# Second tile's norm by halves, one weight chunk reordered, and the input tokens issued on ScalarE's queue

## What is computed

```python
x = layer_norm(ALPHA * x + mix(x), ln_mix_g, ln_mix_b)          # mix: convolutions, then attention
x = layer_norm(ALPHA * x + moe(x), ln_ffn_g, ln_ffn_b)          # 32 experts, top 2 of one group
```

## Time and profile before

| what | value |
|---|---|
| median of 3 runs | 1653.17 us (1652.9 to 1653.77) |
| the profiled execution | 1655.15 us, span of its instructions 1653.4 us |
| mean granted TensorE clock | 0.995 |
| TensorE busy | 1564.0 us, 95% |
| VectorE / ScalarE / GpSimd busy | 482.5 / 266.7 / 72.0 us |
| DMA over the span | 502.48 MB, mean 304 GB/s |

### The profile page before, as it was taken

One profiled execution on the slowest core, in us unless ns is written; L12 is line 12 of the kernel. 1 busy time (PEld: TensorE's weight loads), 2 busy tenths in 40 slices (PEclk: granted clock), 3 DMA queues, 4 the chain that ended last, 5 costly groups with the idle time before them and its releaser, 6 DMA issues.

```text
span 1653.4 us, 25094 instructions
## 1 busy us (share of the span) xinstructions
PE 1564.0 (95%) x10686; PEld 1039.7 (63%) x10686; DVE 482.5 (29%) x934; ACT 266.7 (16%) x667; POOL 72.0 (4%) x138
## 2 busy tenths in 40 slices
PE   9999999998989999999999998898999999999999
PEld 8855555555555676465556555554888678748874
DVE  4951000000000313440000000002436887345652
ACT  1020000000000212210000000001232333322321
POOL 0000000000000000000000000000000431101120
PEclk9999999999999999999999999999999999999999
DMA  9689999999999942499999999999324223324420
GB/s 388 271 326 370 428 427 429 426 430 427 430 427 428 423 165 102 190 421 412 428 428 428 429 427 428 428 427 425 131 109 153 102 103 133 122 102 153 153 102 26
DMA packets 38661, 502.48 MB, mean 304 GB/s; under 512 B 4288, under 2 KB 4544, under 8 KB 6208
## 3 DMA queue, kind: packets, MB, share of 16 engines
q1 hardware_dynamic: 38016, 499.40, 73.3%
q0 software_dynamic: 576, 2.10, 0.3%
HBM read 500.43 MB, written 1.05 MB: 303 GB/s over the span
## 4 chain that ended last, share of the span: by engine, by line
PE 76%; DMA 12%; DVE 7%; issue 2%; ACT 2%; SPq 0%; DVEq 0%; ACTq 0%
PE ps L862 12%; PE ps L885 10%; PE ps L1320 10%; DMA ring<-in_expert_up 9%; PE ps L725 8%; PE ps L948 7%; PE ps L757 6%; PE ps L841 4%; PE ps L907 4%; DMA ring<-in_expert_down 3%; DVE arena L2263 2%; PE ps L1279 2%; PE ps L1107 2%; PE ps L1128 2%; PE ps L1401 1%
## 5 line engine op out<-in xcount | busy, mean ns | idle before, releaser
L862 PE MATMUL ps<-x_tok,tables_sb 128*128 128x256 f32 x1216 | 303.8, 393 | 0.0
L862 PEld LDWEIGHTS ps<-x_tok,tables_sb 128*128 128x128 f32 x1216 | 220.1, 191 | 103.9 <-issue 80.4
L885 PE MATMUL ps<-ring,arena 128*32 128x256 f32 x3968 | 238.6, 382 | 30.4 <-DMA ring<-in_expert_up 20.8
L885 PEld LDWEIGHTS ps<-ring,arena 128*32 128x32 f32 x3968 | 118.8, 110 | 139.0 <-issue 30.9
L725 PE MATMUL ps<-spare,ring 128*128 128x256 f32 x768 | 168.8, 383 | 1.1 <-DVE spare L2140 1.1
L2379 DVE TENSOR_TENSOR arena<-arena,ps 128x128 f32<-128x128 f32 x64 | 18.4, 288 | 497.2 <-ACT arena L1744 497.2
L725 PEld LDWEIGHTS ps<-spare,ring 128*128 128x128 f32 x768 | 147.0, 192 | 21.6 <-DVE spare L2140 1.3
L948 PE MATMUL ps<-ring,arena 128*32 128x512 f32 x928 | 115.6, 615 | 15.9 <-ACT arena L1739 11.3
L1320 PE MATMUL ps<-ring 128*128 128x256 f32 x480 | 110.6, 384 | 0.0
L1320 PEld LDWEIGHTS ps<-ring 128*128 128x128 f32 x480 | 89.8, 190 | 17.1 <-issue 5.5
L757 PE MATMUL ps<-ring,arena 128*128 128x512 f32 x224 | 98.6, 595 | 1.1 <-DVE arena L2315 0.6
(11 more groups left out here) (301 smaller groups left out, 1397.5 us busy)
## 6 DMA issues: line engine op xcount, KB each, us to landing
ring<-in_expert_up SPq DMA_DIRECT2D x124, 2048.0 KB, 20.6
ring<-in_stream SPq DMA_DIRECT2D x43, 2048.0 KB, 8.2
ring<-in_expert_down SPq DMA_DIRECT2D x42, 2048.0 KB, 24.1
ring<-in_expert_down SPq DMA_DIRECT2D x32, 1024.0 KB, 22.3
arena<-in_expert_up SPq DMA_DIRECT2D x4, 2048.0 KB, 11.2
arena<-in_expert_down SPq DMA_DIRECT2D x2, 2048.0 KB, 12.6
tables_sb<-in_expert_down SPq DMA_DIRECT2D x2, 2048.0 KB, 10.0
spare<-in_expert_down SPq DMA_DIRECT2D x2, 2048.0 KB, 10.3
```

Source lines behind the costliest of these rows:

```text
L862: pe.matmul(ps[:, b, 0:TOK], ident, x[:, 0, 0:TOK], start=True, stop=True, skip_group_check=True)
L885: ins = pe.matmul(ps[q * SLOTS:(q + 1) * SLOTS, 4 + e % 2, 0:TOK] .rearrange("p (g n) -> p g n", g=2), xg[:, 4 * half + k, e * SLOTS:(e + ...
```

## The change

- The two transfers of x are issued by ScalarE's queue, ahead of its other work, and no longer by SyncE's.
- In MOE1's opening order chunk 4 stands before chunk 10.
- CONV and STICK raise `half_done` when the first 512 columns of tile 1's output are summed; STICK's last three k-steps run first for these columns, then for the others. In CONV the order of matmuls stays.
- `layer_norm` of these stages takes tile 1's first half's statistics at that signal, and then does the passes over tile 1 by halves of 512 columns: subtract and gain, root, scale and bias of the first half, then of the second.
- In the expert stages the last two transposes of tile 1 (channel blocks 6 and 7) go to bank 4; VectorE copies 256 columns of bank 3, and ScalarE 256 of bank 4, in place of VectorE's 512.

```diff
@@ -178,8 +178,10 @@
         place_of[g], loads_of[g], before_in[g] = b, loaded[b], held.get(b)
         held[b] = g
 
-    halves = [(n, what) for n, what in ((CONV, "out"), (MOE0, "first"), (MOE0, "last"),
-                                        (STICK, "out"), (MOE1, "first"), (MOE1, "last"))
+    halves = [(n, what) for n, what in ((CONV, "out"), (CONV, "summed"),
+                                        (MOE0, "first"), (MOE0, "last"),
+                                        (STICK, "out"), (STICK, "summed"),
+                                        (MOE1, "first"), (MOE1, "last"))
               if n in on]
 
     def half_no(stage, what):
@@ -498,8 +500,6 @@
         @block.sync
         def _(sp):
             sp.dma_start(con[:, 0:P], a["tables"][:, 0:P]).then_inc(x_in, 16)
-            sp.dma_start(x[:, 0, :], a["x"][0][0:P, :]).then_inc(x_in, 16)
-            sp.dma_start(x[:, 1, :], a["x"][0][P:, :]).then_inc(x_late_in, 16)
 
             def load(g, src):
                 if before_in[g] is not None:
@@ -518,7 +518,7 @@
                 if stage == MOE0:
                     order = (7, 0, 1, 2, 3, 6, 8, 10, 4, 5, 9, 11)
                 else:
-                    order = (0, 1, 2, 3, 6, 10, 4, 7, 8, 5, 9, 11)
+                    order = (0, 1, 2, 3, 6, 4, 10, 7, 8, 5, 9, 11)
                 half = SLOT_WORDS // 2
                 for j in order:
                     if j == QUAD_CHUNKS - 1:
@@ -692,15 +692,18 @@
 
         @block.tensor
         def _(pe):
-            def transposes(name, src, ready=lambda t, kk: None, tiles=(0, 1), at=range(4)):
+            def transposes(name, src, ready=lambda t, kk: None, tiles=(0, 1), at=range(4),
+                           last_two=None):
 
                 for b in [2 * t + kk for t in tiles for kk in range(2)]:
                     t, kk = b // 2, b % 2
                     ready(t, kk)
                     for j in range(4):
                         k = 4 * kk + j
-                        ins = pe.transpose(bank(at[b])[:, j * P:(j + 1) * P],
-                                           src[:, t, k * P:(k + 1) * P], ident)
+                        o = bank(at[b])[:, j * P:(j + 1) * P]
+                        if k >= 6 and t and last_two is not None:
+                            o = bank(last_two)[:, (k - 6) * P:(k - 5) * P]
+                        ins = pe.transpose(o, src[:, t, k * P:(k + 1) * P], ident)
                     ins.then_inc(transposed, 1)
 
             def wait_T(name, n=4):
@@ -816,8 +819,11 @@
                 output_tile(g + 5, 2, cv_mixT, 0, 0, parts=(1,)).then_inc(sem("half_done"), 1)
                 output_tile(g + 5, 2, cv_mixT, 0, 1)
                 pe.wait_ge(sem("cv_mixed"), 4)
-                output(g + 5, 2, cv_mixT, 1,
-                       lambda c, t: pe.wait_ge(sem("residual_in"), t + 1))
+                pe.wait_ge(sem("residual_in"), 1)
+                output_tile(g + 5, 2, cv_mixT, 1, 0)
+                pe.wait_ge(sem("residual_in"), 2)
+                output_tile(g + 5, 2, cv_mixT, 1, 1, parts=(0,)).then_inc(sem("half_done"), 1)
+                output_tile(g + 5, 2, cv_mixT, 1, 1, parts=(1,))
 
             def norm_rows(layer, which):
 
@@ -1013,7 +1019,7 @@
                 router(0)
                 wait_x(pe, stage, (0,))
                 residual(0, 0)
-                transposes(name, x, normed(stage), (1,))
+                transposes(name, x, normed(stage), (1,), last_two=4)
                 router(1).then_inc(sem("logits"), 1)
                 residual(0, 1)
                 wait_x(pe, stage, (1,))
@@ -1115,7 +1121,7 @@
                     if q == 3:
                         ins.then_inc(chunk_done, 1)
 
-                def out(t, k):
+                def out(t, k, parts=(0, 1)):
                     c = k // 4
                     if k == 0:
                         pe.wait_ge(sem("sk_taken"), 6 if t == 0 else 3)
@@ -1124,7 +1130,7 @@
                     arrive(pe, g + 6 + c)
                     pe.wait_ge(sem("sk_oT"), k + 1)
                     w = slot4[slot(g + 6 + c)]
-                    for n in range(2):
+                    for n in parts:
                         ins = pe.matmul(bank(STICK_OUT[t] + n), sk_mixT[:, k, t * P:(t + 1) * P],
                                         w[:, k % 4, n * 512:(n + 1) * 512], start=(k == 0),
                                         stop=(k == KT - 1), skip_group_check=True)
@@ -1254,7 +1260,10 @@
 
                 out(0, 7).then_inc(tile_out, 1)
                 for k in (5, 6, 7):
-                    ins = out(1, k)
+                    ins = out(1, k, (0,))
+                ins.then_inc(sem("half_done"), 1)
+                for k in (5, 6, 7):
+                    ins = out(1, k, (1,))
                 ins.then_inc(chunk_done, 1)
 
             projected = [0]
@@ -1640,6 +1649,8 @@
 
         @block.scalar
         def _(act):
+            act.dma_start(x[:, 0, :], a["x"][0][0:P, :]).then_inc(x_in, 16)
+            act.dma_start(x[:, 1, :], a["x"][0][P:, :]).then_inc(x_late_in, 16)
             step = Steps(act, "act_step")
             roots = [0]
 
@@ -1768,9 +1779,12 @@
                 move_T(f"x{stage}", xT, banks=(0, 1))
                 if stage != first:
                     root(1, 1)
-                move_T(f"x{stage}", xT, banks=(2,), moved=sem("router_fed"))
-                act.wait_ge(sem("router_fed"), layer_no(stage))
-                act.sem_inc(moved_T, 1)
+                name = f"x{stage}"
+                move_T(name, xT, banks=(2,), moved=sem("router_fed"))
+                act.wait_ge(transposed, 4 * turn[name] + 4)
+                act.activation(xT[:, 6:8, P:TOK],
+                               bank(4)[:, 0:TOK].rearrange("p (k c) -> p k c", k=2),
+                               ACT.Copy).then_inc(moved_T, 1)
                 act.wait_ge(sem("exp_arg"), 2 * layer_no(stage) - 1)
                 act.activation(ge, ge_m, ACT.Exp).then_inc(sem("exp_out"), 1)
                 act.wait_ge(sem("exp_arg"), 2 * layer_no(stage))
@@ -2198,8 +2212,14 @@
                         dve.wait_ge(chunk_done, base[stage] + STAGE_CHUNKS[stage])
 
                 def statistics(t):
-                    for n in range(2) if mixer else (1,):
-                        half_statistics(at, t, n)
+                    if mixer and t:
+                        dve.wait_ge(sem("half_done"), half_no(stage, "summed"))
+                        half_statistics(at, t, 0)
+                        arrived(t)
+                        half_statistics(at, t, 1)
+                    else:
+                        for n in range(2) if mixer else (1,):
+                            half_statistics(at, t, n)
                     step.settle()
                     step.run(dve.bn_aggr(mv[:, t, :], stats[:, t].rearrange("p n s -> p (n s)")))
                     begun[t] = root_begin(rstd[:, t], mv[:, t, 1:2], 1.0, LN_EPS, t)
@@ -2247,12 +2267,21 @@
                     arrived(1)
                     statistics(1)
                     scaled(0)
+                    centred(1)
+                    scaled(1)
                 else:
                     scaled(0)
-                    arrived(1)
                     statistics(1)
-                centred(1)
-                scaled(1)
+                    for n in range(2):
+                        part = x[:, 1, n * 512:(n + 1) * 512]
+                        step.run(dve.scalar_tensor_tensor(
+                            part, bank(at[1] + n), mv[:, 1, 0:1],
+                            lnr[:, 0, n * 512:(n + 1) * 512], sub, mul))
+                        if n == 0:
+                            root_end(rstd[:, 1], begun[1], 1)
+                        dve.scalar_tensor_tensor(part, part, rstd[:, 1, 0:1],
+                                                 lnr[:, 1, n * 512:(n + 1) * 512], mul, add)\
+                            .then_inc(x_ready[1] if n else sem("x_half"), 1)
 
             def taps(src, dst, w, n, which, bias=None, tiles=range(4)):
 
@@ -2399,7 +2428,10 @@
             def experts(stage, layer):
                 no = layer_no(stage)
                 dve.memset(rankm[:, :, 32:], 0.0).then_inc(sem("padded"), 1)
-                move_T(f"x{stage}", xT, banks=(3,))
+                dve.wait_ge(transposed, 4 * turn[f"x{stage}"] + 4)
+                dve.tensor_copy(xT[:, 4:6, P:TOK],
+                                bank(3)[:, 0:TOK].rearrange("p (k c) -> p k c", k=2))\
+                    .then_inc(moved_T, 1)
                 dve.wait_ge(sem("padded"), no + (first == CONV))
                 dve.wait_ge(sem("logits"), no)
                 lg = ps[:, 6, 0:72].rearrange("p (t n) -> p t n", t=2)
```

## The result

The changed kernel takes 1659.49 us (median of 20 executions, 1654.04 to 1664.91), the kernel before, now with 20 executions too, 1654.70 us (1650.89 to 1659.8). The ratio is 1.0028, 95% interval [1.0019, 1.0037]: 4.6 us slower, between 3.1 and 6.1. I had forecast 0.9 us slower and given slower by over 0.2% a chance of 0.12. The three executions of the kernel before that were shown at first lay within 0.9 us of each other; its twenty lie within 9.

A forecast was written before the change was run, and what follows sets the result against it. TensorE was taken as the bound (76% of the span), with expert weights' DMA setting the rounds once it waits. 1655.15 + 1.0 (late x) - 0.1 (entries) = 1656.05 us, 1654.1 at the median; range 1651.6 to 1657.2.

The forecast's parts named there:

- rival 2: At the start, TensorE idles twice and the first projection may begin at 1.2 GHz: + 3.5, total 1658.0 us; chance 0.12.
- the sum: Whole kernel: 1655.15 us profiled, + 1.0 for late x, - 0.1 for the entries, gives 1656.05; at the median 1654.1.
- The lateness: First projection at the start: 0.1 to 1.8 us late because x comes later; the middle, 1.0 us, taken.
- The bytes: At the start: 2.06 MB must come before x is complete, x having 0.1 MB alone first.
- x's first half would come 0.6 later: At the start, within rival 2: first half about 0.6 us later, second 2 later, so TensorE stands idle twice.
- the lower estimate: At the start: two queues fill the slow start at 0.43 MB a us; projection at 8.9, 0.1 us late.
- The rule of arbitration: At the start: queues alternate row by row; by the skill's packets, 0.8 us in the sum in place of 1.0.
- Entries of the expert stages: First and second expert stage: tile 1's faster norm stays hidden behind TensorE's queue; 0.1 us won for both together.
- Chunk 4: Second expert stage: issued earlier, it fills a gap of the DMA engines, but nobody waits for it; credit 0.
- Rival 1: At the start: x stays first, x and weights come 0.45 us earlier, projection at 8.3, sum 1652.6; chance 0.20.
- Rival 3: First expert stage's end: the slow-clock stretch moves, 2.5 us either way, 1651.6 or 1656.6; chance 0.10.
- The limit of 0.2%: Whole kernel: a measurement tells about 0.2%, 3.3 us, from no change; chance of staying within it 0.84.

The follow-up runs named there:

- e1: Only x's two transfers moved to ScalarE's queue, against the kernel before: ratio 1.0026 [1.0012, 1.0039].

## Why the prediction was wrong

**The step that failed** is in rival 2 and the sum: the clock at the start was put as one rival of 0.12, and it belonged into the sum of the likeliest case. The prediction named the mechanism (x's second half late, TensorE idle twice, the projection at 1.2 GHz), and had what pointed to it: an idle time of some 2 us right behind warming matmuls that themselves ran slow. It then charged the forecast only with the lateness, as if TensorE kept its clock, and gave no reason for the 0.12. Four of four profiles of the changed kernel had the lower clock, and keeping TensorE busy in the gaps brought the ratio from 1.0028 to 1.0005. Its price was too high for the clock, + 3.5 against 1.6 to 3.1 measured (mean 2.4). That the rival's total comes so close (4.8 us over the kernel before; measured 4.6) is in part luck. The range ended at 1657.2 because it left that rival out.

**The lateness** was mis-sized by little. The term was 1.0 within 0.1 and 1.8; the start came 1.28 late in the first profile and 1.5 on average, the transposes behind the gap being slower in two of the four (1.27 and 1.69 us for eight, against 1.09). The prediction also took a later start to reach the expert stage's end undiminished. It does so up to the waits for weights near 525 us; behind them some 0.6 to 0.7 us are lost again (table above), and why stays open. The bytes were overestimated: 2.06 MB were to be moved before x is complete, but q10 moved its last row before 7.5 us, when 7.5 x 0.244 = 1.83 MB had gone; from there to TensorE's start at 8.17 is landing. x had 0.41 MB moved by 4 us nearly alone, not the 0.1 that the prediction took, because the tables and weights moved only 0.07 MB from 2 to 4 us. Two queues did speed the start up (384 GB/s from 4 to 8 us, against 310), a little less than the 430 that the lower estimate took. Wrong was that x's first half would come 0.6 later: it landed 0.7 earlier, and its transposes start at 4.94, right behind the warming records, 0.17 earlier than before.

**The rule of arbitration.** The Trainium skill, "DMA: Bandwidth & Descriptors", section "Queues, rings and completion order", has an engine finish a packet of several descriptors before it turns to another queue. With eight rows of x per engine in one go, x would have been complete with 1.64 MB moved, an estimate of about 7 us by the rates above. The trace has the last row of x between 7.0 and 7.5 us, with 1.83 MB moved at 7.5, and nearly equal shares of the two queues from 4 to 6.5 us. That fits alternation row by row, as in the earlier trace rows, better than packets of many rows, but the trace does not keep the 16 engines apart, so the rule is not settled. The section "Issuing engines are not separate DMA queues" says that issuing from several engines saves only the time of issuing; the runs agree. In the change SyncE issued the first piece 0.93 us earlier (1.20 against 2.13) and it bought nothing; with one half of x on each queue the time saved shows as a projection 0.5 to 0.7 us earlier.

**Entries of the expert stages.** Right: the first half 0.84 us earlier (0.8 forecast), the second 0.1 (0.1), the root behind ScalarE's copies, and all of it hidden but for 0.13 and 0.11 us (0.1 forecast for both together). The smaller copy of bank 3 won nothing that shows: the router still follows the transposes at once. **Chunk 4** came 4.8 us earlier and nobody was waiting.

**Rival 1** (x stays first, 0.20) falls: both queues moved 1 MB in the same 6 us. **Rival 3** happened in the profile and was priced too high: the stretch of 10.2 us at the first expert stage's end became one of 3.4, as in most other profiles. The rival put half of the stretch at 2.5 us; the comparison above puts two thirds of it at 0.5 to 0.7. Stretches later in the kernel cost their full half (from the last statistics of the second expert stage to the end 499.1 us without one, 500.8 with one of 3.4 us) and differ from execution to execution in kernels of both kinds. **The limit of 0.2%** for telling a time from no change was too small for single executions: the three known lay within 0.9 us, twenty of the same kernel spread over 9. Open remain the exact share of the clock (by the kernels with idle matmuls 2.3 and 3.8 us, by the projections 2.4, by the table of stages 2.7), why e1's profile kept its clock, and the 1.0007 of the rest of the change, which may be nothing.

## What to carry to other kernels

A transfer that is needed first has to stay ahead in the queue of what is needed later: moved to a second queue, x was issued 0.45 us sooner and its second half landed 1.7 us later, because it shared the engines with the weights that had stood behind it. Count the bytes that must pass before it is complete, not the time of its issue. And where TensorE has just begun to run and a wait of a microsecond or two is added, as here, put the lower clock into the sum, not among the accidents; or give it matmuls to do in the gap.

## What the runs showed of the hardware that was not expected

- Two queues at the start moved more than one: from 4 to 8 us 374 to 386 GB/s in the six profiles with x on ScalarE's queue, 353 to 369 with one half on each, 310 to 341 in the five with one queue.
- Idle times of only 1.4 to 2.1 us before and 0.8 us behind eight transposes went with 1.2 GHz in four of four profiles of the changed kernel, and not in the one of e1; with five idle matmuls in them the projection ran at 2.4 GHz in both kernels tried.
- The projection's 64 records took 14.05 us at 2.4 GHz and up to 17.14 behind the gap: the clock stayed low for 3.2 to 6.2 us after the projection had begun, while TensorE was busy throughout.
